# Block 2's head roots with tokens on the partitions, in eight columns, turned back by transposes

## The reference

```python
def _rmsnorm(x, g):
    x32 = x.astype(jnp.float32)
    y = x32 * lax.rsqrt(jnp.mean(x32 * x32, axis=-1, keepdims=True) + EPS)
    return (y * g.astype(jnp.float32)).astype(x.dtype)
...
        q_a = _rmsnorm(q_a.reshape(b, s, NKV_A, NQ_A // NKV_A, HEAD_DIM), qn_a[l])
        k_a = _rmsnorm(k_a.reshape(b, s, NKV_A, HEAD_DIM), kn_a[l])
...
        o_d = _diff_blocked(q_d, k_d, v_d.reshape(b, s, NKV_D, 2 * DIFF_DIM), lam, DIFF_DIM ** -0.5)
        o_d = (_rmsnorm(o_d, subln_d[l]) * (1.0 - lam_init)).reshape(b, s, NQ_D * 2 * DIFF_DIM)
```

## Time and profile before

| | us |
|---|---|
| median of 3 runs | 1511.02 (1509.38 to 1514.3) |
| the profiled execution | 1511.78 |
| its span | 1510.0 |
| PE busy | 1417.6 (94%) |
| DVE busy | 856.4 (57%) |
| ACT busy | 729.1 (48%) |
| POOL busy | 384.7 (25%) |

### The profile page before, as it was taken

How to read it: one execution, slowest core, us unless ns; L and a number is a source line. 1 busy time by engine, 2 the same in 40 slices (tenths; PEclk the granted TensorE clock), 3 DMA queues, 4 the chain that set the end, 5 groups by cost and what they waited for, 6 DMA issues and landing times.

```text
span 1510.0 us, 21577 instructions
## 1 busy us (share of the span) xinstructions
PE 1417.6 (94%) x8202; PEld 1102.2 (73%) x8202; DVE 856.4 (57%) x1553; ACT 729.1 (48%) x1557; POOL 384.7 (25%) x273
## 2 busy tenths in 40 slices
PE   7999999999989999999988889999789989999697
PEld 6767677778987677787778856677568856677476
DVE  3655436466662653455577665457665475558655
ACT  3555447555244554555554544435544544436443
POOL 2232132246132322223553211412002112321001
PEclk9999999999999999999989999999999999999999
DMA  6413451226242221112255523511223422521211
GB/s 226 112 30 88 109 137 32 62 69 217 98 154 57 58 84 57 56 46 63 79 205 167 126 57 71 119 57 60 78 64 93 126 59 44 115 66 61 84 56 57
DMA packets 195373, 135.76 MB, mean 90 GB/s; under 512 B 91590, under 2 KB 185414, under 8 KB 195270
## 3 DMA queue, kind: packets, MB, share of 16 engines
q1 hardware_dynamic: 191494, 120.22, 28.9%
q10 hardware_dynamic: 3776, 14.16, 2.5%
HBM read 122.03 MB, written 12.32 MB: 89 GB/s over the span
## 4 chain that ended last, share of the span: by engine, by line
PE 74%; DVE 13%; ACT 7%; issue 2%; DMA 2%; POOL 1%; SPq 1%; ACTq 0%; DVEq 0%; POOLq 0%
PE pb L1487 19%; PE pb L1489 17%; PE pb L1488 17%; PE pb L1570 6%; PE pb L1509 6%; PE pb L1548 4%; ACT prob L1626 2%; ACT tmp L1626 2%; DVE wl L1993 1%; ACT wh L1645 1%; DVE prob L2245 1%; DVE xl L2000 1%; DMA wr<-w_out 1%; PE pb L1520 1%; PE pb L1557 1%
## 5 line engine op out<-in xcount | busy, mean ns | idle before, releaser
L2386 POOL TENSOR_TENSOR wl<-wr,wh 128x512 fp32r<-128x512 f32 x178 | 255.2, 1434 | 874.5 <-ACT wh L1645 870.6
L1487 PE MATMUL pb<-xh,wl 128*128 128x512 f32 (+1 forms) x880 | 354.4, 403 | 11.6 <-DVE xl L2000 8.4
L1489 PE MATMUL pb<-xh,wh 128*128 128x512 f32 (+1 forms) x880 | 327.0, 372 | 0.0
L1488 PE MATMUL pb<-xl,wh 128*128 128x512 f32 (+1 forms) x880 | 326.7, 371 | 0.0
L1993 DVE TENSOR_TENSOR wl<-wr,wh 128x512 fp32r<-128x512 f32 x208 | 165.8, 798 | 165.7 <-ACT wh L1645 165.3
L1645 ACT CAST wh<-wr 128x512 fp32r<-128x512 f32 (+1 forms) x386 | 219.4, 604 | 38.8 <-PE pb L1489 26.3
L1487 PEld LDWEIGHTS pb<-xh,wl 128*128 128x128 f32 x880 | 168.9, 192 | 77.5 <-issue 43.1
L1489 PEld LDWEIGHTS pb<-xh,wh 128*128 128x128 f32 x880 | 168.5, 191 | 29.5
L1488 PEld LDWEIGHTS pb<-xl,wh 128*128 128x128 f32 x880 | 169.7, 193 | 21.7 <-issue 3.2
L1487 PE MATMUL pb<-wh,xl 128*128 128x256 f32 x448 | 133.6, 298 | 16.5 <-DVE wl L1993 7.9
L1626 ACT ACTIVATE prob<-prob,small 128x512 f32<-128x512 f32 (+3 forms) x128 | 76.2, 596 | 138.7 <-DVE small L2208 138.5
(11 more groups left out here) (197 smaller groups left out, 2456.4 us busy)
## 6 DMA issues: line engine op xcount, KB each, us to landing
wr<-w_in SPq DMA_DIRECT2D x39, 1024.0 KB, 5.2
wr<-w_out SPq DMA_DIRECT2D x14, 1024.0 KB, 5.3
wr<-w_in SPq DMA_DIRECT2D x48, 256.0 KB, 4.6
wr<-w_branch SPq DMA_DIRECT2D x48, 128.0 KB, 2.3
x<-prob SPq DMA_DIRECT2D x12, 512.0 KB, 3.3
wr<-w_out SPq DMA_DIRECT2D x48, 128.0 KB, 3.0
wr<-w_mem_kv SPq DMA_DIRECT2D x4, 1024.0 KB, 5.6
prob<-x ACTq DMA_DIRECT2D x2, 2048.0 KB, 11.0
```

The source lines that it names most:

```text
L1487: e.matmul(ps, ll, rh, start=start, stop=False)
L1488: e.matmul(ps, lh, rl, start=False, stop=False)
L1489: t = e.matmul(ps, lh, rh, start=False, stop=stop)
L2386: t = e.tensor_tensor(wl[:, j % 2, c0:c1], wr[:, j % 2, c0:c1], wh[:, j % 2, c0:c1].bitcast(F32), ALU.subtract)
```

## The change

The squares' sums are taken with the tile of squares as the stationary operand, 128 tokens at a time, against two columns of `bones`: the result is 128 tokens on the partitions by two heads, for four groups of tokens eight columns in all. ACT's `Ln` and `Exp` and the first two Newton operations work on 128x8. The third Newton operation reads its operands broadcast over the 64 columns of each head and writes a 128x512 tile with tokens on the partitions. Four PE transposes (new steps `qspread`, `dspread`) turn it back into a PSUM bank, which DVE's multiplication then reads. `qroot` is new as a step of ACT and DVE, and `qspread` stands four yields behind it. For D the corrected root comes one yield before `dspread`, as the steps of `out_diff` had it. The bank is held until the multiplication, and the planner's cost of the sums step goes from 860 to 436 ns.

```diff
-    if k in ("rturn", "vturn", "feat"):
+    if k in ("rturn", "vturn", "feat", "qspread", "dspread", "qsquares", "dsquares"):
         return 436
...
             if br == "A":
                 b = GR[0].take()
-                put("qsquares", l=l, n=n, b=b, sq=sq)
+                put("qsquares", b=b, sq=sq)
                 yield
-                tn = TN.take()
-                put("qnormed", l=l, n=n, b=b, sq=sq, tn=tn, src=tm)
-                give(b, tn, sq)
+                rs = RS.take()
+                put("qroot", b=b, rs=rs, sq=sq)
+                give(rs)
+                for _ in range(4):
+                    yield
+                put("qspread", b=b, sq=sq)
+                put("qnormed", l=l, n=n, b=b, src=tm)
+                give(b, sq)
...
             def scaled():
-                held.append(GR[0].take())
-                put("dsquares", l=l, c=c, b=held[0], ta=ta)
+                held.extend((GR[0].take(), RS.take()))
+                put("dsquares", b=held[0], rs=held[1], ta=ta)
 
             def corrected():
-                tn = TN.take()
-                put("dnewton", l=l, c=c, b=held[0], ta=ta, tn=tn)
-                give(held[0], tn)
+                put("dnewton", b=held[0], rs=held[1], ta=ta)
 
             def gated():
-                put("dsplit", l=l, c=c, ta=ta)
-                give(ta)
+                put("dspread", b=held[0], ta=ta)
+                put("dsplit", l=l, c=c, b=held[0])
+                give(*held, ta)
...
-                t = e.matmul(bank(b), C("bones"), tm(sq), start=True, stop=True)
-                t.then_inc(aux.sem, aux.mark(b))
+                for i in range(4):
+                    t = e.matmul(bank(b)[:, 2 * i:2 * i + 2], tm(sq)[:, 128 * i:128 * i + 128], C("bones")[:, 0:128:64],
+                                 start=True, stop=True)
+                t.then_inc(aux.sem, aux.mark(("sums", b), ("sums", sq)))
+            elif k in ("qspread", "dspread"):
+                b, x = s["b"], s["sq"] if k == "qspread" else s["ta"]
+                w.wait_ge(v_fn, v_fn.at(("root", x)))
+                for i in range(4):
+                    c = slice(128 * i, 128 * i + 128)
+                    t = e.transpose(bank(b)[:, c], tm(x)[:, c], C("ident"))
+                t.then_inc(aux.sem, aux.mark(b, ends=(x,)))
...
+        def newton_heads(rs, v, to):
+
+            x, o = rootx[:, :], root_of(rs)
+            e.scalar_tensor_tensor(x, v, 64e-6, o, ALU.add, ALU.mult).then_inc(v_fn.sem, v_fn.mark())
+            w.wait_ge(v_fn, v_fn.n)
+            e.scalar_tensor_tensor(x, x, -0.5 / 64, o, ALU.mult, ALU.mult).then_inc(v_fn.sem, v_fn.mark())
+            w.wait_ge(v_fn, v_fn.n)
+            w.wait_ge(aux, aux.at(("sums", to)))
+            wide = [y.rearrange("p (i h) -> p i h", i=4).unsqueeze(3).to_broadcast([P, 4, 2, 64]) for y in (x, o)]
+            t = e.scalar_tensor_tensor(tm(to).rearrange("p (i h c) -> p i h c", i=4, h=2), wide[0], 1.5, wide[1], ALU.add, ALU.mult)
+            t.then_inc(v_fn.sem, v_fn.mark(("root", to), ends=(rs,)))
+            w.wait_ge(v_fn, v_fn.n)
...
-                w.wait_ge(a_fn, a_fn.at(("root", s["sq"])))
-                newton_wide(x, bank(s["b"]), 64, s["tn"])
-                s["b"].ended[v_fn] = v_fn.n
-                t = e.tensor_tensor(k_ if n == 2 else q_[:, n, :], src, x, ALU.mult)
+                w.wait_ge(aux, aux.at(b))
+                t = e.tensor_tensor(k_ if n == 2 else q_[:, n, :], src, bank(b), ALU.mult)
```

More of the change, by code:

```diff
@@ L295 @@
 FUNCTIONS = {"gate": (TANHS, GATES), "sqk": (GATES,), "qk": (LOGS, TANHS), "dqk": (LOGS, TANHS), "mtanh": (TANHS, GATES)}
-FUNCTIONS.update((k, (LOGS,)) for k in ("rroot", "qnormed", "dsquares", "norm_x", "rms1", "foxgate"))
+FUNCTIONS.update((k, (LOGS,)) for k in ("rroot", "qroot", "dsquares", "norm_x", "rms1", "foxgate"))
 FUNCTIONS["lambdas"] = (LOGS, TANHS)
@@ L319, in plan @@
     ER, TT = Ring([Slot(i) for i in range(4)]), Ring([Slot(i) for i in range(4)])
-    SM = Ring([Slot(i) for i in range(3)])
+    SM, RS = Ring([Slot(i) for i in range(3)]), Ring([Slot(0), Slot(1)])
     st = {"i": 0, "split": 0, "load": 0, "hold": False, "spread": -1}
@@ L1221, in build @@
     stats = sb("stats", [P, 4, 36])
+    roots, rootx = sb("roots", [P, 2, 8]), sb("rootx", [P, 8])
     banks = [ctx.enter_context(nc.psum_tensor(f"pb{i}", [P, S], F32)) for i in range(8)]
@@ L1246, in sm, with root_of @@
         return small[:, use.slot.i, c:c + n]
+    def root_of(use):
+        return roots[:, use.slot.i, :]
     def gated(use):
@@ L1907, in scalar_program @@
                 t.then_inc(a_fn.sem, a_fn.mark(("square", s["sq"]), ends=(s["b"],)))
[L1908 to L1911, removed]
+            elif k in ("qroot", "dsquares"):
+                w.wait_ge(aux, aux.at(("sums", s["b"])))
+                for g, v in s["rs"].free():
+                    w.wait_ge(g, v)
+                x = root_of(s["rs"])
+                act(x, bank(s["b"])[:, 0:8], ACT.Ln, 1.0 / 64, C("eps6")).then_inc(a_fn.sem, a_fn.mark())
                 w.wait_ge(a_fn, a_fn.n)
-                act(x, x, ACT.Exp, -0.5).then_inc(a_fn.sem, a_fn.mark(("root", s["sq"])))
+                act(x, x, ACT.Exp, -0.5).then_inc(a_fn.sem, a_fn.mark(("root", s["rs"])))
             elif k == "vcopy":
@@ L2308, in vector_program @@
             elif k == "qnormed":
-                l, n, x, src = s["l"], s["n"], tm(s["sq"]), tm(s["src"])
+                l, n, b, src = s["l"], s["n"], s["b"], tm(s["src"])
                 q_, k_, _ = QKV["A"]
-                w.wait_ge(a_fn, a_fn.at(("root", s["sq"])))
-                newton_wide(x, bank(s["b"]), 64, s["tn"])
-                s["b"].ended[v_fn] = v_fn.n
-                t = e.tensor_tensor(k_ if n == 2 else q_[:, n, :], src, x, ALU.mult)
-                t.then_inc(v_fn.sem, v_fn.mark(("paired", l, "A", n), ends=(s["sq"], s["src"])))
+                w.wait_ge(aux, aux.at(b))
+                t = e.tensor_tensor(k_ if n == 2 else q_[:, n, :], src, bank(b), ALU.mult)
+                t.then_inc(v_fn.sem, v_fn.mark(("paired", l, "A", n), ends=(b, s["src"])))
+            elif k in ("qroot", "dnewton"):
+                w.wait_ge(a_fn, a_fn.at(("root", s["rs"])))
+                x = s["sq"] if k == "qroot" else s["ta"]
+                newton_heads(s["rs"], bank(s["b"])[:, 0:8], x)
             elif k == "vturn":
@@ L2342, in vector_program @@
                 t.then_inc(v_fn.sem, v_fn.mark(("dgate", l, c), ends=(s["u"],)))
[L2343 to L2346, removed]
             elif k == "dsplit":
                 l, c = s["l"], s["c"]
-                w.wait_ge(v_fn, v_fn.at(("dnewton", s["ta"])))
+                w.wait_ge(aux, aux.at(s["b"]))
                 w.wait_ge(v_fn, v_fn.at(("dgate", l, c)))
                 z = tmpz[:, :]
-                e.tensor_tensor(z, z, tm(s["ta"]), ALU.mult).then_inc(v_fn.sem, v_fn.mark(("dgated", l, c), ends=(s["ta"],)))
+                e.tensor_tensor(z, z, bank(s["b"]), ALU.mult).then_inc(v_fn.sem, v_fn.mark(("dgated", l, c), ends=(s["b"],)))
                 w.wait_ge(a_hi, a_hi.at(("dsplit", l, c)))
```

8 lines of the change are left out of this document (1 added, 7 removed).

## The result

| | median us (range, runs) | ratio to before [95%] |
|---|---|---|
| before | 1511.02 (1506.81 to 1515.51, 19) | |
| changed | 1517.4 (1509.29 to 1521.63, 19) | 1.0042 [1.0029, 1.0056] |
| changed, again (group 1 below) | 1514.52 (1509.54 to 1519.25, 12) | 1.0026 [1.0012, 1.004] |

The change makes the kernel slower by 0.3 to 0.4%, +6.4 us in the first set of runs and +3.9 in the second. The profiled execution took 1520.07 us with a span of 1518.3. In the changed kernel line 1610 is the rotary product, 1619 the sums, 1627 the transposes of the roots, 1636 those of the values, 1518 queries by keys, 1579 probabilities by values, 1496 to 1498 the products, and 1644 ACT's helper.

A forecast was written before the change was run, and what follows sets the result against it. The prediction took the PE stream, busy 94% of the span, as the bound. Branch A at +4.7 us and branch D at -4.1 gave +0.6 on the median of 1511.02, so 1511.6 us, range 1506 to 1516.5.

The forecast's parts named there:

- the sum of branch D: Branch D, both layers: the changes at c = 0 and c = 1 together save 4.1 us (from -2.4 to -7).
- the sums of c = 0: Branch D: these sums and ACT's work on them lie beside other products, counted as nothing; without that cover +0.2 us.
- c = 1: Branch D, sums to PE's next product: PE bounds it; -1.2 us taken in layer 0, -0.9 in layer 1.
- Branch A, +4.7: Branch A: waits +1.2 and +1.0 us, half clock +1.7 and +0.85, in layers 0 and 1 (from +2.0 to +8).
- Branch D, c = 0: Branch D: the product with the values starts earlier, -1.0 us a layer (none to at most -1.4).
- a shift of a triple by the planner: Tail of D and C: new planner costs shift single triples of fills; taken as nothing, 1 us to either side.
- The sums: PE, each tile: eight records of 0.09 us take 0.72 us (0.36 to 2.6) where the removed product took 0.86.
- The root on DVE: DVE, each tile: root plus gaps take 1.2 us where three wide rows took 2.17.
- the third: Slower: new wait before A's root transposes brings 6 us half-clock stretches in both layers; +5.5 us, 1516.5; chance 0.13.
- The fourth: Sums not narrow in time: uncovered loads of 0.3 us each, 2.6 for 0.86 a tile, some +12 us; chance 0.05.
- the second: Faster: shorter waits in D halve its half-clock stretch, and A has no half clock; -6.5 us, 1504.5; chance 0.16.

The follow-up runs named there:

- group 1: One chip's set of follow-up runs, with the kernel before (1510.61 us) and the changed kernel run a second time (1514.52 us, ratio 1.0026).
- D alone: The changed kernel with branch A put back to its old root, so only branch D is changed: 1511.6 us (1.0013), again 1512.95 us (1.001).
- A alone: The changed kernel with branch D put back to its old root, so only branch A is changed: 1515.85 us, ratio 1.003.
- wide sums in D: Only branch D changed, with 128 moving columns instead of two in each sums product: 1509.72 us (0.9985), again 1508.19 us (0.9981).
- roots first: The changed kernel with branch A's sums and roots ahead of its rotary product and rows: 1505.23 us (0.9962), again 1507.85 us (0.9969).
- first and deferred: As roots first, with D's c = 1 transposes moved behind three products and C's first queries by keys: 1509.0 us, ratio 0.999.

## Why the prediction was wrong

**The step that failed** is the sum of branch D, "-4.1 (from -2.4 to -7)", and in it the sentence that the sums of c = 0 "lie beside other products and count as nothing". As work it was right: D alone does 3.6 and 4.0 us less. But the term held no half clock beyond that of before, and D alone loses 5.4 and 4.9 us more of it. By mean spans D came to +1.7 and +0.9, not -4.1. The prediction had named the length of the half-clock stretches as its least certain term, but priced it in A alone. I had read the earlier trace rows as a price of waits only, and looked for new stretches only where PE would wait longer. The cheap-looking narrow sums, between waits of 1.35 and 0.52 us that were there before, tipped the clock at c = 0 in 12 of 16 places.

The forecast of +0.6 was met by +6.4 and +3.9. The second value lies inside the stated range and the first just outside it, but neither came by the sum as it was made up. The range of D was also too narrow at its poor end: with its own bounds (none for c = 0, -1.0 and -0.4 for c = 1) that is -1.4, not -2.4.

**Branch A, +4.7**: right in size, +4.8 of work and +0.1 of lost clock. Layer 0 came to +2.8 at the values' transposes (889.50 against 886.28, less 0.44 by which PE was already late at the rotary product, 868.61 against 868.17), where I had 1.2 + 1.7. The wait was 2.83, not 3.9: PE reached the transposes later. The stretch of half clock behind it is there, but it takes the place of the one before, which the start at 886.28 already held; so it counts as work here. Layer 1 came to +2.8 behind DVE's root, where I had 1.0 and half of a stretch; this profile has a whole one. The two layers sum to +5.6 in the profile and A alone to +4.9 by mean spans. That the total is so near 4.7 is in part luck, since three of its parts were off: the first wait (2.83 for 3.9), a new wait of 0.55 at n = 2 that the working had at nothing, and layer 1.

**Branch D, c = 0**: from the last eight transposes of probabilities to the product with the values are 1.84 us (1090.36 to 1092.20) instead of 2.99 (1083.73 to 1086.72): -1.15 for -1.0, and PE has no wait there, where I expected one of some 0.5. Missed was +0.35 ahead of it, the wait for ACT that grew from 1.57 to 1.92: nine products of fills stand ahead of it now, twelve before. That is a shift of a triple by the planner, which I had put at nothing.

**c = 1**: 6.5 us from sums to the product that no longer waits for `yl` (1096.95 to 1103.48), for 7.72: -1.2, as predicted, and PE bounds it as argued. In layer 1 it was 7.35 (1434.29 to 1441.64), all at half clock, for 7.09: nothing gained of the predicted 0.9 in this profile.

**The sums**: 0.80 us from start to start at full clock in A, 0.92 in D behind a wait, for the predicted 0.72. The Trainium skill, TensorE: Matmul & The Clock Gate, section "LDWEIGHTS (loading the stationary operand)", gave 0.85 by the load alone, which is an estimate from its figure, and was nearer. The root on DVE took 1.08 us (878.06 to 879.14), for 1.2.

**The rivals.** The time landed near the third, but not by its mechanism: A alone lost no more clock in the mean (+0.1), and its profile has one new stretch, in layer 1, not a 6 us one in both. The fourth is out, since the sums are narrow in time, and so is the second: the long stretch behind c = 1 stayed.

**What stays open**: why wide sums in D still lose 1.1 to 2.9 us more than before, which with 12 runs is hardly clear of nothing. Half clock behind the wait of 1.93 is one place, in some profiles; no run changed that wait alone. That the width of the moving operand costs clock is shown by the pairs in D alone and in roots first, and the profiles put it at c = 0. It raises the chance of a fall and doesn't fix it: two of eight narrow profiles (the first of roots first, and first and deferred) kept full clock there in both layers, while roots first, profiled a second time as the same kernel, did not. What decides it from one execution to the next is not shown. Of the lost clock at c = 1 of layer 1 no run isolates a cause.

## What to carry to other kernels

When an edit puts short products where PE already has waits on both sides, count the clock of what follows as part of its price, and test it by widening the moving operand at equal issue time: here 128 columns for two gave back 2 to 5 us of median in four pairs (clear of the scatter in the two of D alone). Work made smaller is worth little while it stays queued behind a late transfer; moving A's roots ahead of the rotary rows was worth some 9 us against the changed kernel (ratios of 0.9962 and 0.9969 against 1.0026, in different groups). Split an effect of a few us into span times granted clock and the rest before explaining it.

## What the runs showed of the hardware

At c = 0 of branch D the gaps of PE were equal in the narrow and the wide version (1.36 and 0.52 us), and so was the time on PE (0.92 us). Behind eight products with two moving columns the granted clock was at half, 1.2 GHz, in 12 of 16 places, and behind eight with 128 in none of 8. The Trainium skill, TensorE: Matmul & The Clock Gate, section "Why this matters for your kernels", names gaps of PE between bursts as what costs the clock; these rows, with equal gaps, differ by something else. A DVE operation of 128x512 that reads 8 columns broadcast takes 691 ns, as the dense one did (0.68); one of 128x8 takes 0.16 to 0.17 us, and ACT's of 128x8 0.27 and 0.30.
